# Gate and up products of the last block by seven quarter products in place of eight

## The chip, the cores and the metric

The kernel runs on one core of one Trainium2 chip. The metric is the device time in microseconds (us) of one execution. The engines are TensorE (PE; PEld is its weight load), VectorE (DVE), ScalarE (ACT), GpSimd (POOL), and SyncE (SP), which issues the transfers.

## The reference

A transformer layer runs over 2048 prompt tokens and 32 sample tokens; width 1024, hidden width 2816, all in fp32. The part that changes is the feed-forward network:

```python
x1 = _layer_norm(ALPHA * x + mix, ln1_g, ln1_b)
ffn = (jax.nn.silu(x1 @ w_gate) * (x1 @ w_up)) @ w_down
y = _layer_norm(ALPHA * x1 + ffn, ln2_g, ln2_b)
```

Attention, a pooling mix and the output projection come before it.

## The kernel before

**Blocks, pairs, chunks.** The 2048 prompt tokens are four blocks of 512 (BLOCKS, BW); the 32 sample tokens ride with the last block, whose width is 544 (XW). The hidden width is 22 chunks of 128 columns, taken two at a time: 11 pairs (PAIRS), each of chunks e = 0 and e = 1. For a block, x1T holds the transposed x1 (8 slices of 128 along the width, k = 0 to 7, times the tokens).

**Split operands.** TensorE multiplies fp32r numbers. Each fp32 operand is split in two: hi is ScalarE's copy of it, lo is raw minus hi, and a product is three matmuls, hi x hi, hi x lo, lo x hi. The raw tensor and its lo share one place. gate_hi (L1442) makes the hi of gate and up weights (tiles gw, four slots of [128, 8, 128]); gate_lo (L1819, VectorE) makes the lo of the gate weights and up_lo (L2173, GpSimd) that of the up weights; down_hi (L1447) and down_lo (L2178, GpSimd) do it for the down weights (dw, two slots).

**One pair in the last block on TensorE.** gate(b, p, e, g, i) issues the matmuls of gate (g = 0) or up (g = 1) for chunk e in four parts: 8 k, 2 halves of 272 tokens, 3 matmuls, so 48 of 128x272 each, into banks GU_BANK + g (first half) and Z_BANK + g (second). A pair is: gate e0; the ten down groups of the pair before (downs, into two banks that alternate; group d waits for the add of group d - 2); up e0; gate e1; up e1. A down group is 6 matmuls of 512 columns; the last two, for the packed sample tokens, have 4.

**What the other engines do for a chunk.** sigmoid (ScalarE, L1463) writes it to hT's raw; times_gate (L1827) and times_up (L1836) multiply by the two PSUM results (semaphores silu and prod); hidden_hi (L1470) and hidden_lo (L1845, L1847) split it; add_down (L1859) adds each down group to acc. Each is written into its engine's program at a fixed step of the pair; an engine executes its program in order. Up to the start of the last block's feed-forward part, attention and the mix of the next block run in the same steps (background); in the last block there are none. There the second normalization of the block before is spread over pairs 0 to 4: statistics and centring on VectorE (L1764), scaling on ScalarE (L1409), bias on GpSimd (L2154).

**Order of loads.** SyncE issues the gate and up loads (load_gate, 512 KB each) as their slot comes free, and both down loads of a pair after the down groups of the pair before.

**The end.** The last pair has no down groups; in it VectorE runs fold (L1767) and add_fold (L1771), which add up the sample rows. Then last_downs runs the down groups of the last two pairs together, and each tile of tokens is normalized as its sums are complete.

Of the kernel before, what the change touches and what calls it, by code (L numbers as in the profile page):

```python
# [23 lines left out]
P = 128  # L24
# [119 lines left out]
def stream(nc, ctx, sem, sb, passed, bank, ident, ident_r, mask, mask_r, maskd_r, eps_t, qT_d, kT_d, kcT_d, vp_d, vs_d, vc_d,  # L144
# [29 lines left out]
    acc = [sb(ctx, f"acc{u}", [P, BT, D]) for u in range(2)]  # L174
    acc_s = sb(ctx, "acc_s", [P, D])
# [64 lines left out]
    at[0] = 4 * D  # L240
    dw_last, hT_last = [], []
    for u in range(2):
        hi, lo = piece(f"dw_last_hi{u}", (D,)), piece(f"dw_last_lo{u}", (D,))
        dw_last.append([hi, lo, again(f"dw_last_raw{u}", (D,), F32)])
        hi, lo = piece(f"hT_last_hi{u}", (XW + DEC,)), piece(f"hT_last_lo{u}", (XW,))
        hT_last.append([hi, lo, again(f"hT_last_raw{u}", (XW,), F32)])

# [3 lines left out]
    def is_packed(b, p):  # L251
        return b == BLOCKS - 1 and p < PAIRS - 2

# [154 lines left out]
    def x_part(b, x):  # L408
# [43 lines left out]
        sem(f"f_{n}") for n in ("gate_up", "sig", "silu", "prod", "h_hi", "h_lo", "down", "sum"))  # L452
    y_stored, filled = sem("y_stored"), sem("filled")
    last_up, last_prod, last_hi, last_lo = (sem(f"last_{n}") for n in ("up", "prod", "hi", "lo"))
# [150 lines left out]
    def chunks(b):  # L605

        return [(0, BW)] if b < BLOCKS - 1 else [(0, XW // 2), (XW // 2, XW // 2)]

# [15 lines left out]
    with nc.Block() as block:  # L624
        @block.sync
        def _(sp):
# [175 lines left out]
            def load_gate(L):  # L802
# [3 lines left out]
                if P0:  # L806
# [9 lines left out]
            def load_down(b, p):  # L816
                if is_last(b, p):
                    sp.wait_ge(m_sums, mix_count(BLOCKS))
                    sp.wait_ge(folded, 2)
# [149 lines left out]
            for b in range(BLOCKS):  # L969
                for p in range(PAIRS):  # L970
                    pair = PAIRS * b + p
                    more = pair + 1 < PAIRS * BLOCKS
                    for i in range(4):
# [39 lines left out]
        def _(pe):  # L1013
# [196 lines left out]
            def gate(b, p, e, g, i):  # L1210
# [20 lines left out]
                if i == 1 and L == 4 * PAIRS * BLOCKS - 1:  # L1231
                    m.then_inc(last_up, 1)
# [78 lines left out]
            for b in range(BLOCKS):  # L1311
                for p in range(PAIRS):
                    if b + p == 0:
# [28 lines left out]
        def _(act):  # L1342
# [106 lines left out]
            def sigmoid(b, p, e):  # L1449
# [14 lines left out]
                m.then_inc(sig, 1)  # L1464

# [152 lines left out]
            for b in range(BLOCKS):  # L1618
                for p in range(PAIRS):
                    pair = PAIRS * b + p  # L1620
                    more = pair + 1 < PAIRS * BLOCKS
                    for i in range(4):
# [8 lines left out]
                    if p:  # L1631
                        for d in range(2 * tiles_of(b)):
                            background(next(slot))
                    for i in range(4):
# [6 lines left out]
                    for i in range(4):  # L1641
                        background(next(slot))
                        if i == 0 and more:
# [6 lines left out]
                    for i in range(4):  # L1650
# [5 lines left out]
                        if i == 3 and more:  # L1656
# [11 lines left out]
                else:  # L1668
                    for n, (first, w) in enumerate(chunks(b)):
                        if n == 0:  # L1670
                            act.wait_ge(last_prod, 1)
                        else:
                            act.wait_ge(prod, 2 * PAIRS * BLOCKS)
# [19 lines left out]
        def _(dve):  # L1693
# [136 lines left out]
            def times_up(b, p, e):  # L1830
# [6 lines left out]
                m.then_inc(prod, 1)  # L1837

# [489 lines left out]
```

## Time and profile before

| what | us |
|---|---|
| median of 3 runs | 2630.28 |
| lowest and highest | 2629.57, 2630.89 |
| the profiled execution, its own time | 2634.26 |
| its span, first to last instruction | 2632.5 |

Granted TensorE clock over the span: 0.995 of full. A profile shows one execution. Times in rows are us from the start of its span unless marked ns; "idle before <-releaser" is how long the engine had nothing to do before the instruction and what released it. L1227 is the line of the gate and up matmuls, L1259 that of the down matmuls.

### The profile page before, as it was taken

How to read it: one execution, taken by the hardware profiler on the slowest of the kernel's cores; microseconds unless marked ns; L12 is line 12 of the kernel's file. 1: busy time of each engine (PE TensorE's matmuls, PEld its weight loads, DVE VectorE, ACT ScalarE, POOL GpSimd, SP SyncE). 2: the span in 40 equal slices, each digit the busy share in tenths (PEclk: the TensorE clock that was granted, in tenths of full speed). 3: DMA queues.
4: the chain of work that ended last, by engine and by line, in shares of the span. 5: the costliest groups of instructions: out<-in, count | busy, mean ns of one | idle time of the engine just before them, and what ended most of it. 6: DMA issues, size and time to landing. Idle time of an engine off the chain costs nothing.

```text
span 2632.5 us, 37813 instructions
## 1 busy us (share of the span) xinstructions
PE 2559.2 (97%) x14210; PEld 2189.4 (83%) x14210; DVE 1470.4 (56%) x1952; ACT 1115.3 (42%) x1892; POOL 1126.4 (43%) x1013
## 2 busy tenths in 40 slices
PE   8999899999999999999999999999999999999998
PEld 8978798788878878778788887878878888999997
DVE  3366336666444366787734567787774354543335
ACT  4365326565232135566532265656554123322213
POOL 3465436755223135456621274556543124242223
PEclk9999999999999999999999999999999999999999
DMA  6697956764446233444254234333524512223222
GB/s 227 191 271 248 330 176 193 222 212 127 133 131 232 82 111 109 124 113 120 77 201 155 89 113 116 101 116 101 167 74 144 176 62 97 89 73 128 89 81 83
DMA packets 211013, 373.92 MB, mean 142 GB/s; under 512 B 30768, under 2 KB 105136, under 8 KB 208784
## 3 DMA queue, kind: packets, MB, share of 16 engines
q1 hardware_dynamic: 210832, 371.50, 44.7%
q8 instruction: 114, 1.87, 0.3%
q14 instruction: 67, 0.55, 0.1%
HBM read 303.34 MB, written 68.09 MB: 141 GB/s over the span
## 4 chain that ended last, share of the span: by engine, by line
PE 84%; DVE 5%; issue 3%; DMA 3%; POOL 2%; ACT 2%; SPq 1%; ACTq 0%; POOLq 0%; DVEq 0%
PE bank L1227 35%; PE bank L1259 19%; PE bank L1177 8%; PE bank L1136 7%; PE bank L1036 5%; PE bank L1083 4%; PE bank L1052 4%; DMA gw_lo_raw<-in_w_in_dram 2%; DVE left L1725 1%; PE bank L1159 1%; POOL gw_lo L2187 1%; DMA v_st<-v_cache_scratch 1%; DMA mixT<-mixT_scratch 0%; ACT bank L1375 0%; ACT beta L1374 0%
## 5 line engine op out<-in xcount | busy, mean ns | idle before, releaser
L1227 PE MATMUL bank<-x1T,gw_hi 128*128 128x512 f32 (+1 forms) x3488 | 930.2, 355 | 4.8 <-DVE hT_lo_raw L1827 3.4
L1227 PEld LDWEIGHTS bank<-x1T,gw_hi 128*128 128x128 f32 x3488 | 600.7, 189 | 85.9 <-issue 4.5
L1227 PE MATMUL bank<-x1T,gw_lo 128*128 128x512 f32 (+1 forms) x1744 | 614.4, 352 | 0.0
L2146 POOL TENSOR_TENSOR beta<-beta,left 128x512 f32<-128x512 f32 (+2 forms) x326 | 350.0, 1074 | 362.6 <-DVE left L1725 361.9
L2173 POOL TENSOR_TENSOR gw_lo<-gw_lo_raw,gw_hi 128x1024 fp32r<-128x1024 f32 x88 | 223.6, 2540 | 588.3 <-ACT gw_hi L1442 588.1
L1725 DVE TENSOR_TENSOR_SCAN left<-bank,left,zero_t 128x512 f32<-128x512 f32 (+2 forms) x326 | 363.9, 1116 | 74.7 <-ACT bank L1375 69.1
L1177 PE MATMUL bank<-x1T,gw_hi 128*128 128x256 f32 (+2 forms) x1472 | 355.7, 334 | 13.9 <-DVE x1T L1946 8.8
L1227 PEld LDWEIGHTS bank<-x1T,gw_lo 128*128 128x128 f32 x1744 | 328.4, 188 | 46.9
L1859 DVE TENSOR_TENSOR acc<-bank,acc 128x512 f32<-128x512 f32 x312 | 213.6, 686 | 260.4 <-PE bank L1259 260.1
L1365 ACT ACTIVATE aT<-bank 128x512 fp32r<-128x512 f32 (+2 forms) x326 | 173.7, 533 | 434.1 <-PE bank L1052 385.3
L1716 DVE TENSOR_TENSOR aT<-bank,aT 128x512 fp32r<-128x512 f32 (+2 forms) x326 | 196.9, 604 | 202.5 <-ACT aT L1365 201.1
L1259 PE MATMUL bank<-dw_hi,hT_hi 128*128 128x512 f32 x728 | 295.1, 405 | 8.7 <-issue 7.3
L2178 POOL TENSOR_TENSOR dw_lo<-dw_lo_raw,dw_hi 128x1024 fp32r<-128x1024 f32 x86 | 212.4, 2470 | 201.0 <-ACT dw_hi L1447 200.9
L1259 PE MATMUL bank<-dw_lo,hT_hi 128*128 128x512 f32 x728 | 287.2, 394 | 0.0
L1177 PEld LDWEIGHTS bank<-x1T,gw_hi 128*128 128x128 f32 x1472 | 245.2, 191 | 34.4 <-issue 11.7
L1259 PE MATMUL bank<-dw_hi,hT_lo 128*128 128x512 f32 x692 | 273.4, 395 | 0.0
L1463 ACT ACTIVATE hT_lo_raw<-bank 128x512 f32<-128x512 f32 (+1 forms) x106 | 53.3, 522 | 481.8 <-PE bank L1259 368.8
L1177 PE MATMUL bank<-x1T,gw_lo 128*128 128x256 f32 (+2 forms) x736 | 243.3, 331 | 0.0
L1036 PE MATMUL bank<-k_st,q_st 128*128 128x512 f32 (+3 forms) x688 | 215.5, 383 | 8.9 <-DVE left L1725 6.9
L2187 POOL TENSOR_TENSOR gw_lo<-gw_lo_raw,gw_hi 128x1024 fp32r<-128x1024 f32 x58 | 142.1, 2450 | 191.8 <-ACT gw_hi L1483 185.8
L1136 PE MATMUL bank<-wo_hi,mixT 128*128 128x256 f32 x1056 | 204.3, 285 | 3.8 <-DMA mixT<-mixT_scratch 3.7
L1083 PE MATMUL bank<-aT,v_st 128*128 128x512 f32 (+3 forms) x640 | 185.3, 371 | 0.0
(177 smaller groups left out, 3749.4 us busy)
## 6 DMA issues: line engine op xcount, KB each, us to landing
gw_lo_raw<-in_w_gate_dram SPq DMA_DIRECT2D x88, 512.0 KB, 3.6
gw_lo_raw<-in_w_up_dram SPq DMA_DIRECT2D x88, 512.0 KB, 3.6
dw_lo_raw<-in_w_down_dram SPq DMA_DIRECT2D x86, 512.0 KB, 4.4
gw_lo_raw<-in_w_in_dram SPq DMA_DIRECT2D x64, 512.0 KB, 4.5
k_st<-kT_scratch SPq DMA_DIRECT2D x160, 128.0 KB, 4.0
v_st<-v_scratch SPq DMA_DIRECT2D x80, 256.0 KB, 4.2
q_st<-qT_scratch SPq DMA_DIRECT2D x128, 128.0 KB, 3.9
wo_raw<-in_w_out_dram SPq DMA_DIRECT2D x16, 1024.0 KB, 5.6
```

Source lines behind the costliest of these rows:

```text
L1036: m = pe.matmul(z, q_st[queries.slot][:, j, who * P:(who + 1) * P], k_st[slot][:, 0:it.width], start=h == 0 and j == 0, stop=last)
L1083: m = pe.matmul(out[:, cols], v_st[held[0].slot][:, u - it.macro, :], aT[u % 2][j][:, cols], start=opens_group(u) and j == 0, stop=closes_ ...
L1136: x = pe.matmul(bank[Z_BANK + j % 2][:, 0:QW], turned[a][:, k, cols_of(t)], weights[c % 2][w][:, k, :], start=k == 0 and a + w == 0, stop= ...
L1177: y = pe.matmul(p_bank(b, n, slice(first, first + w)), weight[:, k, :], x1T[j][:, k, first:first + w], start=k == 0 and x == 0, stop=k == ...
L1227: m = pe.matmul(gu_bank(g, n)[:, 0:w], gw[L % 4][a][:, k, :], x1T[x][:, k, first:first + w], start=k == 0 and s == 0, stop=k == KD - 1 and ...
L1259: m = pe.matmul(bank[D_BANK + index % 2][0:cols.stop - cols.start, :], hid(b, p)[e][a][:, cols], dws(b, p)[e][w][:, half * 512:half * 512 ...
L1716: dve.tensor_tensor(aT[u % 2][1][:, cols], bank[t_at[u]][:, cols], r32(aT[u % 2][0][:, cols]), ALU.subtract).then_inc(aT_lo, 1)
L1725: dve.tensor_tensor_scan(out[:, 0:w][:, ::-1], bank[z_at[n]][:, 0:w][:, ::-1], zero_t[:, 0:1].broadcast_to([P, w]), out[:, w:w + 1], ALU.m ...
L1859: m = dve.tensor_tensor(x, bank[D_BANK + index % 2][:], x, ALU.add)
L2146: pool.tensor_tensor(x[:, 0:w], x[:, 0:w], left[n % RL][:, 1:w + 1], ALU.mult).then_inc(a_done, 1)
L2173: pool.tensor_tensor(gw[L % 4][1][:], gw[L % 4][2][:], r32(gw[L % 4][0][:]), ALU.subtract).then_inc(u_lo, 1)
L2178: pool.tensor_tensor(lo[:], raw[:], r32(hi[:]), ALU.subtract).then_inc(d_lo, 1)
```

## The change

In the last block, pairs 2 to 10 (WINO_FROM = 2; 18 chunks, c = 0 to 17), gate and up of a chunk are computed together as one product of two-by-two blocks: the width of 1024 is cut in TOP and LOWER (4 k each), the tokens in FIRST and SECOND (272 each), and the two outputs are gate and up. Strassen's scheme in Winograd's form takes seven quarter products (4 k x 3 = 12 matmuls of 128x272) instead of eight.

- Sums of weights, on VectorE in fp32 (quarter_sums, 4 instructions of 512 elements a row; one overwrites the top half of the up weights). Three of them fill a new tile, extra. Four weight operands become seven, so per chunk extra_hi (ScalarE, 1536 elements) and extra_lo (VectorE, 1536) are new. The lo of the gate weights goes from VectorE to GpSimd (gate_quarters_lo), except chunk 0's.
- Sums of tokens, once: token_sum, 8 instructions of 4 x 272 elements in pairs 0 and 1, and four splits (tokens_hi, tokens_lo), in part written over x1T.
- Sums of results, on VectorE, PSUM and SBUF to either: copy_part (ScalarE), make_v, make_y, make_up_2, make_up_1, make_gate_2, 272 elements each. Two of the seven products add up on top of others in a bank by accumulation.
- Sigmoid and the multiplies go by halves of 272. Six banks rotate (wino_bank).
- Order on TensorE: seven products of chunk e0, the ten down groups, seven products of e1. In VectorE's program extra_lo(c+1) stands after the add of down group 1, quarter_sums(c+2) after that of group 5, extra_lo(c+2) after that of group 8.
- The last pair's down weights move to where block 2's acc was; load_gate waits on the product that last reads the slot.

```diff
+            def seven_products(c):
+                pe.wait_ge(wg_lo, c + 1)
+                pe.wait_ge(prod, done - 1)
+                quarter(wino_bank(c, GATE_1), g, 0, x1T, 0, FIRST, True).then_inc(seven, 1)
+                pe.wait_ge(wx_lo, c + 1)
+                pe.wait_ge(t_lo, 3)
+                quarter(wino_bank(c, UP_2), s2, 0, xt[2], 0, whole, True).then_inc(seven, 1)
+                pe.wait_ge(wu_lo, c + 1)
+                pe.wait_ge(silu, done)
+                quarter(wino_bank(c, UP_1), u, 0, xt[3], 0, whole, True).then_inc(seven, 1)
+                pe.wait_ge(t_lo, 4)
+                pe.wait_ge(prod, done)
+                quarter(wino_bank(c, GATE_2), s1, 0, x1T, 0, SECOND, True).then_inc(seven, 1)
+                pe.wait_ge(part_copied, c + 1)
+                quarter(wino_bank(c, GATE_1), g, KH, x1T, KH, FIRST, False).then_inc(seven, 1)
+                pe.wait_ge(corner, 5 * c + Y_MADE)
+                quarter(wino_bank(c, UP_1), u, KH, xt[4], 0, whole, False).then_inc(seven, 1)
+                pe.wait_ge(corner, 5 * c + UP_2_MADE)
+                quarter(wino_bank(c, GATE_2), s4, 0, x1T, KH, SECOND, False).then_inc(seven, 1)
...
+            def quarter_sums(c):
+                dve.tensor_tensor(s1, u[:, TOP, :], u[:, LOWER, :], ALU.add).then_inc(s_sums, 1)
+                dve.tensor_tensor(u[:, TOP, :], g[:, TOP, :], u[:, TOP, :], ALU.subtract).then_inc(s_sums, 1)
+                dve.wait_ge(s_sums, 4 * c + S_1)
+                dve.tensor_tensor(s2, s1, g[:, TOP, :], ALU.subtract).then_inc(s_sums, 1)
+                dve.wait_ge(s_sums, 4 * c + S_2)
+                dve.tensor_tensor(s4, g[:, LOWER, :], s2, ALU.subtract).then_inc(s_sums, 1)
```

VectorE's program for a pair:

```diff
+            def wino_pair(b, p):
+                if c:
+                    make_gate_2(c - 1)
+                    half_times_gate(c - 1, 1)
+                    half_times_up(c - 1, 1)
+                else:
+                    times_up(b, p - 1, 1)
+                    tokens_lo(1, 3)
+                make_v(c)
+                hidden_lo(b, p - 1, 1)
+                make_y(c)
+                make_up_2(c)
+                quarter_sums(c + 1)
+                make_up_1(c)
+                make_gate_2(c)
+                for d in range(2 * tiles_of(b)):
+                    if not is_last(b, p):
+                        add_down(b, p - 1, d)
+                    if d == 1:
+                        extra_lo(c + 1)
+                    if d == 3:
+                        for group in range(4):
+                            for i in range(4):
+                                second_norm(b, p, group, i)
+                    if d == 5 and not is_last(b, p):
+                        quarter_sums(c + 2)
+                    if d == 8 and not is_last(b, p):
+                        extra_lo(c + 2)
+                if is_last(b, p):
+                    dve.wait_ge(summed, downs_done(b, PAIRS - 3))
+                    fold(3)
+                    add_fold(3)
+                half_times_gate(c, 0)
+                half_times_gate(c, 1)
+                half_times_up(c, 0)
+                half_times_up(c, 1)
+                make_v(c + 1)
+                hidden_lo(b, p, 0)
+                make_y(c + 1)
+                make_up_2(c + 1)
+                half_times_gate(c + 1, 0)
+                make_up_1(c + 1)
+                half_times_up(c + 1, 0)
```

GpSimd's:

```diff
+            def wino_pair(b, p):
+                if c == 0:
+                    up_quarters_lo(0)
+                gate_quarters_lo(c + 1)
+                up_quarters_lo(c + 1)
+                for group in range(4):
+                    for i in range(4):
+                        second_norm(b, p, group, i)
+                if not is_last(b, p):
+                    gate_quarters_lo(c + 2)
+                    up_quarters_lo(c + 2)
+                for e in range(2):
+                    down_lo(PAIRS * b + p, e)
```

ScalarE's:

```diff
+            def wino_pair(b, p):
+                if c:
+                    half_sigmoid(c - 1, 1)
+                else:
+                    tokens_hi(1)
+                copy_part(c)
+                hidden_hi(b, p - 1, 1)
+                gate_quarters_hi(c + 1)
+                up_quarters_hi(c + 1)
+                extra_hi(c + 1)
+                for group in range(4):
+                    for i in range(4):
+                        second_norm(b, p, group, i)
+                if more:
+                    gate_quarters_hi(c + 2)
+                    up_quarters_hi(c + 2)
+                    extra_hi(c + 2)
+                half_sigmoid(c, 0)
+                half_sigmoid(c, 1)
+                copy_part(c + 1)
+                hidden_hi(b, p, 0)
+                down_hi(pair, 0)
+                down_hi(pair, 1)
+                half_sigmoid(c + 1, 0)
```

On GpSimd gate_quarters_lo(c) waits for the fourth sum of c (S_4), up_quarters_lo(c) for up_quarters_hi(c), which waits for the second (S_3); extra_hi(c) waits for the fourth, extra_lo(c) for extra_hi(c). In pair 1, quarter_sums(0) stands before times_gate of e1 on VectorE, and extra_lo(0) and gate_quarters_lo(0) near the end of the pair.

## Rows read from the trace of the kernel before

**Rows 1.** The page's first part: busy time, share of the span, count of each engine
```profile
PE 2559.2 (97%) x14210; PEld 2189.4 (83%) x14210; DVE 1470.4 (56%) x1952; ACT 1115.3 (42%) x1892; POOL 1126.4 (43%) x1013
```

**Rows 2.** The chain of waits, last block, in order: start, us, what
```profile
2503.97 13.13 PE bank L1259 x56
...
2517.10 24.11 PE bank L1227 x192
...
2596.52 27.92 PE bank L1259 x120
```

**Rows 3.** Timeline, VectorE and weight loads, down groups: start, us, what, idle before
```profile
2513.76 0.69 DVE L1859 TENSOR_TENSOR acc<-bank,acc 128x512 f32<-128x512 f32 x1 [0.70 <-PE bank L1259]
...
2515.15 0.69 DVE L1859 TENSOR_TENSOR acc<-bank,acc 128x512 f32<-128x512 f32 x1 [0.70 <-PE bank L1259]
...
2517.14 0.69 DVE L1859 TENSOR_TENSOR acc_s<-bank,acc_s 128x512 f32<-128x512 f32 x1 [0.35 <-PE bank L1259]
...
2515.90 0.19 PEld L1259 LDWEIGHTS bank<-dw_hi,hT_hi 128*128 128x128 f32 x1 [0.28 <-DVE acc L1859]
```

**Rows 4.** One line's instructions each: ns min/median/max, first and last start, shapes
```profile
L1819 DVE TENSOR_TENSOR gw_lo<-gw_lo_raw,gw_hi x88: 1171/1218/3422, 563.6 to 2574.9; 128x1024 fp32r<-128x1024 f32 x88
...
L1859 DVE TENSOR_TENSOR acc<-bank,acc x312: 655/691/695, 661.6 to 2618.9; 128x512 f32<-128x512 f32 x156
...
L1836 DVE TENSOR_TENSOR hT_lo_raw<-bank,hT_lo_raw x40: 428/436/442, 2225.3 to 2572.8; 128x272 f32<-128x272 f32 x40
...
L1442 ACT ACTIVATE gw_hi<-gw_lo_raw x42: 1044/1060/1064, 2212.2 to 2579.0; 128x1024 fp32r<-128x1024 f32 x42
...
L1463 ACT ACTIVATE hT_lo_raw<-bank x40: 391/396/399, 2219.3 to 2566.7; 128x272 f32<-128x272 f32 x40
```

**Rows 5.** Timeline, VectorE: two pairs of instructions that follow each other
```profile
2387.80 0.69 DVE L1845 TENSOR_TENSOR hT_lo<-hT_lo_raw,hT_hi 128x512 fp32r<-128x512 f32 x1 [0.73 <-ACT hT_hi L1470]
...
2388.41 0.19 DVE L1847 TENSOR_TENSOR hT_hi<-hT_lo_raw,hT_hi 128x32 fp32r<-128x32 f32 x1
...
2600.75 0.69 DVE L1859 TENSOR_TENSOR acc<-bank,acc 128x512 f32<-128x512 f32 x1 [2.81 <-PE bank L1259]
...
2601.47 0.69 DVE L1746 BATCH_NORM_STATS2 stats<-acc 128x6 f32<-128x512 f32 x1
```

**Rows 6.** Timeline, GpSimd (POOL), where it meets VectorE
```profile
562.57 1.09 POOL L2146 TENSOR_TENSOR beta<-beta,left 128x512 f32<-128x512 f32 x1 [4.42 <-DVE left L1725]
...
2265.06 2.41 POOL L2178 TENSOR_TENSOR dw_lo<-dw_lo_raw,dw_hi 128x1024 fp32r<-128x1024 f32 x1 [2.24 <-ACT dw_hi L1447]
...
2270.29 3.26 POOL L2178 TENSOR_TENSOR dw_lo<-dw_lo_raw,dw_hi 128x1024 fp32r<-128x1024 f32 x1 [2.82 <-ACT dw_hi L1447]
...
2309.89 2.40 POOL L2173 TENSOR_TENSOR gw_lo<-gw_lo_raw,gw_hi 128x1024 fp32r<-128x1024 f32 x1
...
2312.26 5.19 POOL L2154 TENSOR_TENSOR acc<-acc,bias 128x1024 f32<-128x1024 f32 x2
```

**Rows 7.** Timeline, VectorE (DVE), the same stretches and the last pair's fold
```profile
561.21 1.28 DVE L1725 TENSOR_TENSOR_SCAN left<-bank,left,zero_t 128x512 f32<-128x512 f32 x1 [0.29 <-ACT bank L1375]
...
2265.09 3.45 DVE L1764 SCALAR_TENSOR_TENSOR acc<-acc,mv,gain 128x1024 f32<-128x1024 f32 x1
...
2313.35 1.85 DVE L1845 TENSOR_TENSOR hT_lo<-hT_lo_raw,hT_hi 128x512 fp32r<-128x512 f32 x1 [0.72 <-ACT hT_hi L1470]
...
2315.13 2.37 DVE L1847 TENSOR_TENSOR hT_hi<-hT_lo_raw,hT_hi 128x32 fp32r<-128x32 f32 x1
...
2580.74 3.29 DVE L1771 TENSOR_TENSOR acc_s<-acc_s,low_rows 32x1024 f32<-32x1024 f32 x1
```

**Rows 8.** The page's DMA issues: KB each, median us from issue to landing
```profile
gw_lo_raw<-in_w_gate_dram SPq DMA_DIRECT2D x88, 512.0 KB, 3.6
```

**Rows 9.** Timeline, ScalarE, end of pair 1 of the last block
```profile
2268.58 0.69 ACT L1463 ACTIVATE hT_lo_raw<-bank 128x272 f32<-128x272 f32 x2 [3.60 <-PE bank L1227]
...
2269.15 1.06 ACT L1447 ACTIVATE dw_hi<-dw_lo_raw 128x1024 fp32r<-128x1024 f32 x1
```

More of the change, by code:

```diff
@@ L1230, in gate, with quarter @@
                     m.then_inc(gate_up, 1)
-                if i == 1 and L == 4 * PAIRS * BLOCKS - 1:
-                    m.then_inc(last_up, 1)
+            def quarter(out, weights, at_k, moving, at_x, cols, first):
+                for k in range(KH):
+                    for s, (a, x) in enumerate(((0, 0), (0, 1), (1, 0))):
+                        m = pe.matmul(out, weights[a][:, at_k + k, :], moving[x][:, at_x + k, cols],
+                                      start=first and k == 0 and s == 0, stop=k == KH - 1 and s == 2, skip_group_check=True)
+                return m
+            def seven_products(c):
+                pair, e, _ = chunk_of(c)
+                done = 2 * pair + e
+                g, u = gw[2 * e], gw[2 * e + 1]
+                s1, s2, s4 = ([extra[e][j][:, x, :, :] for j in range(2)] for x in range(3))
+                whole = slice(0, HW)
+                pe.wait_ge(wg_lo, c + 1)
[16 more added lines that the diff above has]
+                quarter(wino_bank(c, GATE_2), s4, 0, x1T, KH, SECOND, False).then_inc(seven, 1)
             def first_gate_and_up(i):
@@ L1655, in _ @@
                             down_hi(pair, 1)
-                        if i == 3 and more:
+                        if i == 2 and before_wino:
+                            up_quarters_hi(0)
+                            extra_hi(0)
+                        elif i == 3 and not before_wino:
                             gate_hi(4 * pair + 5)
@@ new lines, in make_gate_2, with half_of, half_times_gate @@
+            def make_gate_2(c):
+                dve.wait_ge(seven, 7 * c + P3)
+                dve.tensor_tensor(wino_bank(c, GATE_2), wino_bank(c, GATE_2), part[:], ALU.add).then_inc(corner, 1)
+            def half_of(c, half):
+                pair, e, _ = chunk_of(c)
+                return hid(*divmod(pair, PAIRS))[e][2][:, (FIRST, SECOND)[half]]
+            def half_times_gate(c, half):
+                h = half_of(c, half)
+                dve.wait_ge(half_sig, 2 * c + half + 1)
+                dve.tensor_tensor(h, wino_bank(c, (GATE_1, GATE_2)[half]), h, ALU.mult).then_inc((half_silu, silu)[half], 1)
@@ L2048, in _ @@
                             times_up(b, p, 0)
-                        if i == 1 and more:
+                        if i == 1 and not before_wino:
                             gate_lo(4 * pair + 4)
```

251 lines of the change are left out of this document (222 added, 29 removed).

## The prediction

> **What bounds the kernel now.** I read the page first: TensorE is busy for 97% of the span [rows 1]. Then the chain of waits over the last block, where the change lies: it is matmuls end to end, 24.11 us for the 192 gate and up matmuls of a pair, 13.13 us for the 56 down matmuls, to 2624.4 us, where the tail of normalization begins [rows 2]. So 0.1256 us a gate or up matmul (24.11 / 192), and any matmul taken out comes off the time, unless TensorE then waits. Third, the timeline of VectorE, ScalarE and GpSimd in one pair, for what the new work costs and between which matmuls it falls. A down group of six matmuls takes 1.39 us (2513.76 to 2515.15), and only the tenth waits: its weights came 0.06 us after the add two groups back ended, about 0.1 us of matmul went with it (what the sum below leaves), and its own add began 1.30 us after that add's end [rows 3]. That is about 0.15 us a pair (13.13 against 8 x 1.39 + 2 x 0.93), and the pattern I price the new stalls by.
>
> **What the change takes from TensorE.** Seven products of 12 matmuls stand for 96 matmuls: 84 x 0.1256 = 10.55 us a chunk, one product 1.507 us, 1.51 us less a chunk, 3.01 us a pair, 27.1 us over nine pairs. The matmul's shape and its weights' shape stay, so the row's price holds. Waits stand in front of all seven; down groups have one each and lose nothing by it [rows 3].
>
> **What it adds.** Prices [rows 4, 5]: a VectorE add or subtract of 1024 elements 1.22 us, of 512 0.69 us (the next instruction starts 0.08 to 0.09 us before its end, if it needs nothing from it; 0.03 us after it, if it does), so 1536 about 1.75 us (estimate, same slope); corner sums of 272 from PSUM 0.44 us; ScalarE 1.06 us for 1024, about 1.5 us for 1536, 0.4 us for 272. Per pair VectorE gets 8 quarter sums, 10 corner sums, two splits of 1536, and loses one gate split. ScalarE and GpSimd (now 6 splits of 2.4 us, some 14 us) have room in a pair of 37 us; VectorE, some 26 us, too. Loads land 3.6 us after issue [rows 8], and each has over 4 us. What matters is order.
>
> **Inside a pair, steady state.** Zero is the first product of chunk c (e = 0); products end at 1.51, 3.01, 4.52, 6.03, 7.53, 9.04, 10.55. The corner sums stay ahead: the end of the chunk before (last corner sum, sigmoid, two multiplies, 0.2 + 0.44 + 0.4 + 0.44 + 0.44 and latencies) is through at 2.1, wanted at 4.5; make_y ends at 5.2, wanted at 7.5; make_up_2 ends at 6.7, wanted at 9.0. quarter_sums(c+1) runs from 6.57: 0.60 + 0.60 + 0.72 + 0.69 = 2.61, to 9.18.
>
> Then ten down groups, from 10.55, with only two PSUM banks: group d cannot start before the add of group d-2.
> - After add 1, extra_lo(c+1), 1.75 us: add 1 starts at 2 x 1.39 + 0.20 = 2.98 behind the start of the groups, the split at 3.58, add 2 at 5.24 and ends at 5.93. Group 4 wants to start at 5.56: with 0.06, and the 0.1 of matmul, as in [rows 3], a stall of 0.53.
> - After add 5, quarter_sums(c+2), 2.61 us. From the end X of group 5: add 5 X+0.20 to X+0.89, sums from X+0.80 to E = X+3.41, add 6 to E+0.60; group 8 wanted to start at X+2.78 and does at E+0.77: 1.40.
> - The old wait of 0.15 before group 9 goes.
> Without anything else a pair so changes by -3.01 + 0.53 + 1.40 - 0.15 = -1.23 us.
>
> **The shared lock.** GpSimd and VectorE exclude each other where VectorE has two inputs in SBUF. At 2313.35 such a subtract met a GpSimd add begun at 2312.26: it took 1.85 us for 0.69 and ended at 2315.20, so the add let go 2.2 us after its start; the waiting second GpSimd add then got in before VectorE's next instruction, which took 2.37 us for 0.18 [rows 6, 7]. Adds from PSUM never show it: 655 to 695 ns in 312 of them, against up to 3422 ns for the split of the same kind from SBUF [rows 4]. So no two instructions overlap here, and the one that waits is next. The Trainium skill says this too (SBUF — State Buffer, section SBUF: two separate sides): an exclusive lock, whoever starts first keeps it for its whole instruction; the trace agrees, with these durations. By a reading in which both merely ran side by side, the sum would be the third rival's.
>
> Who meets whom: at E the fourth sum of c+2 frees GpSimd's gate_quarters_lo(c+2), 0.08 us later (561.21 + 1.28 to 562.57) [rows 6, 7]; its up_quarters_lo(c+2) follows 2.37 us behind (2309.89 to 2312.26): E+2.45. On VectorE add 6 ends at E+0.60, add 8 starts 1.30 later at E+1.90, extra_lo(c+2) at E+2.50. GpSimd is first by 0.05 us. A lead of 0.03 us was enough at 2265.06 against 2265.09: 3.45 us, 2.2 more than 1024 elements take [rows 4, 6, 7]. Then extra_lo(c+2) runs from E+2.45+2.2 = E+4.65 to E+6.4, add 9 to E+7.0, the two half_times_gate to E+7.69. TensorE began chunk c+1 at E+2.63, and its third product, which waits for silu of chunk c, wants to start at E+5.64 and does at E+7.86: 2.22. The pair is then -1.23 + 2.22 = +0.99 us. If VectorE comes first, the multiplies end at E+5.5 and this wait is nought: those are the bounds, and I take GpSimd first, by these rows. The other meetings are clear: extra_lo(c+1) at 14.13 finds up_quarters_lo(c+1) letting go at 13.84; down_lo and hidden_lo miss each other.
>
> **Once each.**
> - Pairs 3 and 4: a GpSimd bias add follows directly on up_quarters_lo(c+1), at 14.00, before extra_lo(c+1) at 14.13: 2.1 us each, and in pair 3 the third bias add still touches the quarter sums (0.1): +4.3. Bounds 0 and 8.6 (a second meeting in each).
> - Entry (pair 1 to 2): wg_lo of chunk 0 is VectorE's last work, behind extra_lo(0), behind extra_hi(0), behind up_quarters_hi(0), behind down_hi, which ended at 2270.2 [rows 9]. Clear of locks: 2270.2 + 1.0 + 1.5 + 1.66 + 1.22 = 2275.6, where the first product could start at 2274.4 (the sigmoid of the chunk began at 2268.58, 0.2 after the last matmul before [rows 9]; + 6.0): 1.2. The two down_lo (one at 2270.29 [rows 6]) and up_quarters_lo(0) fall among quarter_sums, centre and extra_lo: up to three holds of 2.2, so 1.2 to 7.8; I take two, 5.6. The token sums lie in stretches with over 3 us of VectorE idle and cost nothing; were they late, add 1 or add 6 of pair 1 would be by up to 0.5.
> - Last pair: no down groups between its chunks, so the cover is gone. The gate split of c+1, moved to GpSimd, starts at 9.26 and ends at 11.66, wanted at 10.55: 1.3. extra_lo waits for it to 11.46, ends at 13.2; up_quarters_lo, waiting, holds to 15.3; then fold 0.7 and add_fold about 1.25 (3.29 before, which I read as a hold of 2.0 [rows 7]; an estimate) and two multiplies to 18.1, where product 3 wants 14.84: 3.4. So -3.01 + 4.7 = +1.7. Without locks -0.8.
> - The end: first columns' last_lo is ready 0.6 us after the last product, wanted 2.8 us after; the other half 3.5 against 11. Nothing.
>
> **Sum:** 8 pairs x 0.99 = 7.9, + 4.3 + 5.6 + 1.7 = +19.5 us. On the profiled execution, span 2632.5 us and 2634.26 us as a time: 2652.0 and 2653.8. The median of the runs is 4.0 lower, 2630.28; there 2649.8.
>
> **Rivals.**
> 1. VectorE first at E+2.5 in all pairs: 8 x -1.23 = -9.8, + 11.6: +1.8, 2632.1. Against it only 0.05 us of lead, worked out from latencies of 0.01 us grain. If it flips from pair to pair, anything between.
> 2. More meetings than I placed (both bias adds twice, three holds at the entry, hidden_lo behind a down_lo): 7.9 + 8.6 + 7.8 + 1.7 = +26, with one hold more in a few pairs +30: 2660.
> 3. Faster: the lock doesn't take these instructions (operands of [P, 4, 128] slices, or a hold much under 2.2 us). Place: every SBUF split and sum. 8 x -1.23 + 1.2 - 0.8 = -9.4: 2620.9. It decides from a hold of under about 0.1 us at E+2.45; [rows 6, 7] speak against it.
> 4. TensorE waits nowhere: -27.1, 2603.2. Needs VectorE's 2.61 us of sums to fit in 0.5 us of slack before group 8. Almost excluded.
>
> **How the numbers follow.** Forecast 0.55; rival 1 0.20; rival 2 0.10; rival 3 0.12; rival 4 0.03. 0.2% (5.3 us) is about what this kernel's runs can tell from no change. Slower: 0.55 + 0.10 + 0.03 of rival 1 = 0.68; faster: 0.12 + 0.03 = 0.15; within: 0.17. The range, 2627 to 2656, leaves out rivals 3 and 4 and most of 2 and takes in rival 1; the forecast's own is 2643 to 2656 (entry and bias adds at their bounds).
>
> **What would show it.** Per quarter product 12 matmuls in 1.5 us. A wait of TensorE for VectorE before groups 4 and 8 of each pair, some 0.5 and 1.4 us. VectorE's 1536-element split after the ninth add at 3.9 us where the other of the pair takes 1.75, and TensorE's third product of odd chunks released by the multiply of the even one. A pair of 38.2 us; 36.0 if rival 1 is right. I am wrong if that split is at 1.75 us throughout, or if GpSimd's second split starts after it.

## The result and the profile after

Before: 2630.28 us median (2629.57 to 2630.89). After: 2645.66 us median of five (2639.09 to 2648.51). The ratio of the executions is 1.0054, 95% interval 1.0039 to 1.0070: slower. Between the medians it is 15.4 us, where +19.5 was forecast.

The profiled execution of after is the fastest of the five, 2639.09 us. Its page, first part:

```profile
span 2637.2 us, 37777 instructions
...
PE 2541.1 (96%) x13994; PEld 2166.2 (82%) x13994; DVE 1583.2 (60%) x2127; ACT 1156.8 (44%) x1932; POOL 1186.9 (45%) x1030
```

Against [rows 1] TensorE has 216 matmuls fewer (18 x 12) and 18.1 us less work, VectorE 112.8 us more. 18 and not 27 us: a part of TensorE's time has become longer, some of it by a lower clock (below).

The chain of waits, last block, the matmul stretches in order: start, us, what. First three rows of the kernel before that [rows 2] lacks, then after's:

```profile
2213.23 30.14 PE bank L1227 x240
...
2256.48 24.11 PE bank L1227 x192
...
2554.33 42.19 PE bank L1227 x336
```

```profile
2208.19 30.13 PE bank L1285 x240
...
2276.12 12.16 PE bank L1293 x84
...
2303.21 21.22 PE bank L1293 x168
...
2342.91 21.23 PE bank L1293 x168
...
2381.26 21.23 PE bank L1293 x168
...
2526.00 21.23 PE bank L1293 x168
...
2562.16 21.23 PE bank L1293 x168
...
2601.28 27.88 PE bank L1347 x120
```

The block begins at 2213.2 before and at 2208.2 after, in code that the change doesn't touch; over all later runs it lies between 2209.9 and 2216.7. So I compare within the block (the last block's feed-forward part and the tail behind it), from its first row to the end of the span: 2632.5 - 2213.2 = 419.3 us before, 2637.2 - 2208.2 = 429.0 us after. This execution lost 9.7 us in the block, and the rows say where:

| stretch | before | after | lost |
|---|---|---|---|
| block start to first product of chunk 0 | 61.3 | 67.9 | +6.6 |
| first product of chunk 0 to that of chunk 2 | 37.23 | 37.7 | +0.5 |
| the next pair (3) | 37.23 | 39.70 | +2.5 |
| pair 4 | 37.23 | 38.35 | +1.1 |
| pairs 5 to 9 | 186.2 | 180.9 | -5.3 |
| last pair, first product to last downs | 24.11 | 28.51 | +4.4 |

(Before, 144 matmuls of each row of 192 or 336 belong to the pair before, so its starts are 2256.48 + 18.1 and 2554.33 + 18.1; 37.23 is a row of 24.11 and one of 13.13 in [rows 2]. After, a row of 168 is the odd chunk of one pair and the even one of the next, so the last pair begins at 2562.16 + 10.61 = 2572.77.)

What TensorE waited for, from its timeline of after: the entry (the first product, chunk 0's), the two groups of a steady pair, and the two waits of the last pair. The number in brackets is the idle time before, then what ended it:

```profile
2276.12 0.82 PE L1293 MATMUL bank<-x1T,gw_hi 128*128 128x272 f32 x2 [6.55 <-DVE gw_lo L2035]
...
2516.92 0.51 PE L1347 MATMUL bank<-dw_hi,hT_hi 128*128 128x512 f32 x1 [0.26 <-DVE acc L2175]
...
2523.89 0.50 PE L1347 MATMUL bank<-dw_hi,hT_hi 128*128 128x512 f32 x1 [1.12 <-DVE acc L2175]
...
2584.45 0.52 PE L1293 MATMUL bank<-x1T,gw_hi 128*128 128x272 f32 x2 [1.07 <-POOL gw_lo L2506]
...
2591.02 0.57 PE L1293 MATMUL bank<-xt_hi,gw_hi 128*128 128x272 f32 x1 [3.19 <-DVE hT_last_raw L2094]
```

Those at 2516.92 and 2523.89 are groups 4 and 8, where the prediction put them. No row has the multiply L2094 in front of the third product of an odd chunk: in this execution the wait that carried 17.8 of the forecast's 19.5 us didn't occur once. Here is the meeting in the pair of the second and third row, VectorE's and GpSimd's timelines:

```profile
2522.54 0.69 DVE L2029 TENSOR_TENSOR extra_raw<-gw_lo_raw,extra_raw 128x512 f32<-128x512 f32 x1
...
2525.72 1.75 DVE L2040 TENSOR_TENSOR extra_lo<-extra_raw,extra_hi 128x1536 fp32r<-128x1536 f32 x1
```

```profile
2523.37 2.41 POOL L2506 TENSOR_TENSOR gw_lo<-gw_lo_raw,gw_hi 128x1024 fp32r<-128x1024 f32 x1 [8.89 <-DVE extra_raw L2029]
2525.73 4.00 POOL L2511 TENSOR_TENSOR gw_lo<-gw_lo_raw,gw_hi 128x1024 fp32r<-128x1024 f32 x1
```

VectorE's extra_lo(c+2) starts 0.01 us ahead and runs its 1.75 us; GpSimd's up_quarters_lo(c+2) is recorded at 4.00 us for 2.40, because it waits. It is a tie, and all eight pairs of this execution are like it. GpSimd starts 0.14 us after the fourth sum's end (2523.23), where I had taken 0.08.

The table's rows hide one thing more, the granted clock. In these rows it is the number behind the POOL entry (1.00 is full); first around the entry, then around the last wait:

```profile
2262.00:2269.00 7.00, 7.00 (x58) 7.00 (x57) 6.65 (x5) 2.70 (x4) 6.34 (x3) 1.00 0.27 75
...
2276.00:2278.00 2.00, 1.88 (x8) 1.88 (x9) 1.96 (x4) 0.00 (x0) 0.00 (x0) 0.50 0.00 0
...
2280.00:2284.00 4.00, 4.00 (x34) 4.00 (x34) 1.79 (x5) 1.14 (x2) 0.00 (x0) 1.00 0.02 4
```

```profile
2591.00:2593.00 2.00, 1.98 (x9) 2.00 (x10) 1.62 (x4) 1.40 (x2) 0.00 (x0) 0.50 0.00 0
2593.00:2596.00 3.00, 3.00 (x15) 3.00 (x15) 0.46 (x2) 1.16 (x2) 2.72 (x2) 0.50 0.03 5
```

Behind its wait of 6.55 us TensorE came back at half clock, the lower of the two levels, 1.2 GHz: chunk 0's 84 matmuls took 12.16 us for 10.61, which is why the table's second row reads 37.7 for a steady 36.15. Behind the wait of 3.19 us it was at half until past 2596. The last pair took 28.51 us: 21.11 of products (as where nothing waits, below), 4.26 of the two waits, and 3.1 more, nearly all of it (some 2.7) from 5.5 us at half clock.

The clock also fell in pair 3. TensorE waited 2.45 us before down group 4, where a bias add held the split, and behind it groups 4 and 5 took 4.43 us. In the run with VectorE first (below) the same wait is there and the clock stays at full. After's chain, then that run's:

```profile
2332.45 4.43 PE bank L1347 x12
```

```profile
2335.38 3.07 PE bank L1347 x12
```

Pair 3 is 39.70 us here and 38.50 there, so the clock cost it 1.2 us. Nothing in the prediction accounts for any of the three.

### The profile page after: what moved, and what is told of

The parts are those of the page before. It is cut to its first block, busy times and chain, and to the rows that moved or that the text cites. A ratio compares the mean times of both kernels' runs of the same rounds, so it can differ in the third digit from the quotient of the medians.

```text
span 2637.2 us, 37777 instructions
## 1 busy us (share of the span) xinstructions
PE 2541.1 (96%) x13994; PEld 2166.2 (82%) x13994; DVE 1583.2 (60%) x2127; ACT 1156.8 (44%) x1932; POOL 1186.9 (45%) x1030
## 4 chain that ended last, share of the span: by engine, by line
PE 82%; DVE 7%; issue 4%; DMA 2%; POOL 2%; ACT 2%; SPq 0%; DVEq 0%; POOLq 0%; ACTq 0%
PE bank L1285 27%; PE bank L1347 17%; PE bank L1235 9%; PE bank L1194 7%; PE bank L1293 7%; PE bank L1094 5%; PE bank L1141 4%; PE bank L1110 4%; DVE left L1902 1%; DMA gw_lo_raw<-in_w_in_dram 1%; DVE acc L2175 1%; POOL gw_lo L2540 1%; PE bank L1217 1%; DMA v_st<-v_cache_scratch 1%; DMA mixT<-mixT_scratch 0%
## 5 line engine op out<-in xcount | busy, mean ns | idle before, releaser
L1285 PE MATMUL bank<-x1T,gw_hi 128*128 128x512 f32 (+1 forms) x2336 | 713.1, 389 | 4.8 <-DVE hT_lo_raw L2004 3.4
L1285 PEld LDWEIGHTS bank<-x1T,gw_hi 128*128 128x128 f32 x2336 | 419.3, 189 | 85.2 <-issue 4.5
L1285 PE MATMUL bank<-x1T,gw_lo 128*128 128x512 f32 (+1 forms) x1168 | 448.4, 384 | 0.0
L2500 POOL TENSOR_TENSOR gw_lo<-gw_lo_raw,gw_hi 128x1024 fp32r<-128x1024 f32 x70 | 181.7, 2595 | 427.6 <-ACT gw_hi L1537 427.4
L1235 PEld LDWEIGHTS bank<-x1T,gw_hi 128*128 128x128 f32 x1472 | 244.9, 190 | 32.9 <-issue 10.0
L1285 PEld LDWEIGHTS bank<-x1T,gw_lo 128*128 128x128 f32 x1168 | 220.1, 188 | 47.0
L2540 POOL TENSOR_TENSOR gw_lo<-gw_lo_raw,gw_hi 128x1024 fp32r<-128x1024 f32 x58 | 142.1, 2449 | 186.4 <-ACT gw_hi L1648 182.3
L1347 PEld LDWEIGHTS bank<-dw_hi,hT_hi 128*128 128x128 f32 x728 | 137.8, 189 | 61.8 <-DVE acc L2175 23.9
```

Of the source, the lines that this page charges most:

```text
L1235: y = pe.matmul(p_bank(b, n, slice(first, first + w)), weight[:, k, :], x1T[j][:, k, first:first + w], start=k == 0 and x == 0, stop=k == ...
L1285: m = pe.matmul(gu_bank(g, n)[:, 0:w], gw[L % 4][a][:, k, :], x1T[x][:, k, first:first + w], start=k == 0 and s == 0, stop=k == KD - 1 and ...
L1347: m = pe.matmul(bank[D_BANK + index % 2][0:cols.stop - cols.start, :], hid(b, p)[e][a][:, cols], dws(b, p)[e][w][:, half * 512:half * 512 ...
```

## The experiments

Beside each ratio to before I give the length of the last block in the profiled execution (419.3 before, 429.0 after). Chips and executions differ by a few us ahead of that block, so the block is the sharper measure of a place, and the ratio of the whole. The block is one execution each, though, and holds whatever the clock did in it. Behind the entry's wait alone that was 1.55 to 2.8 us in the seven profiles that have it. The first four runs below ran on one chip, the next four on another, the last on a third; each ratio is to the kernel before on the same chip.

### The changed kernel once more

> The changed kernel once more, unchanged, for the spread of its executions. Theory A (a tie for the shared lock): in the profiled execution VectorE's extra_lo(c+2) and GpSimd's up_quarters_lo(c+2) began within 0.01 us of each other in every pair, and VectorE had the lock each time; each lost tie costs 2.2 us, eight ties an execution, so the executions lie between 2639 and 2657 us, as they did (2639.1 to 2648.5), and differ by several us. Theory B (the spread has another cause: transfers, the clock, the stages before the last block): the same spread here, and it stays when the tie is removed.

Measured: 2649.05 us (2642.72 to 2656.34, six runs), ratio 1.0059, 1.0043 to 1.0074. Block 436.1 us, 7.1 more than in the first profile. One group of TensorE's lines in the last block:

```profile
L1293 PE MATMUL bank<-xt_hi,gw_hi 128*128 128x272 f32 x144 | 43.4, 301 | 9.7 <-DVE hT_lo_raw L2094 6.5 <-DVE hT_last_raw L2094 3.2
```

The 6.5 us for hT_lo_raw are three waits of 2.17, the wait of the forecast at its forecast price (2.22), but in three pairs of eight. In one of them both engines are recorded at the same hundredth:

```profile
2573.01 4.02 DVE L2040 TENSOR_TENSOR extra_lo<-extra_raw,extra_hi 128x1536 fp32r<-128x1536 f32 x1
```

```profile
2573.01 2.40 POOL L2511 TENSOR_TENSOR gw_lo<-gw_lo_raw,gw_hi 128x1024 fp32r<-128x1024 f32 x1
```

This time GpSimd got the lock and VectorE's 1.75 us became 4.02. Same program, other winner: by an estimate of eight times 2.17, that puts up to 17 us of chance on top of the few us by which executions of the kernel before differ too (2629.91 to 2637.53 in 19 runs of this chip).

### The tie decided for VectorE, and for GpSimd

For VectorE, in GpSimd's program:

```diff
                     gate_quarters_lo(c + 2)
+                    pool.wait_ge(wx_lo, c + 3)
                     up_quarters_lo(c + 2)
```

> GpSimd's up_quarters_lo(c+2) waits until extra_lo(c+2) is done, so VectorE is always first; no work is removed. Theory A: all executions near the fastest of the changed kernel, 2639 us, within 1.5 us of each other, ratio to before 1.0033. Theory B: median still about 2645 and a spread of 9 us.

For GpSimd, in VectorE's program:

```diff
                     if d == 8 and not is_last(b, p):
+                        dve.wait_ge(wu_lo, c + 3)
                         extra_lo(c + 2)
```

> VectorE's extra_lo(c+2) waits until up_quarters_lo(c+2) is done, so GpSimd is always first. Theory A: the third product of each odd chunk of pairs 2 to 9 starts some 2.4 us late (2.2 of the lock and 0.2 more, since the wait is for the end and not for the release), 8 x 2.4 = 19 us over the run before: 2658 us, small spread. Theory B: no more than the changed kernel's own 2645, since the slack behind the split hides it.

Measured, VectorE first: 2641.54 us (2639.19 to 2646.49, seven runs), ratio 1.0031, 1.0021 to 1.0041, block 428.0. GpSimd first: 2670.23 us (2665.31 to 2675.56, four runs), ratio 1.0132, 1.0117 to 1.0147, block 457.1. The first has the expected ratio (1.0033), and its interval and that of the undecided kernel don't meet. But its executions spread over 7.3 us, not 1.5: undecided it was 13.6 us, and the kernel before has 7.6 on this chip, so some 6 us of the spread point to the tie (few executions), and the rest has another cause. The second went the expected way but cost 28.7 us over the first, not the 19 expected of eight waits, and it spread over 10 us, not little. Its lines, its chain in two successive pairs, and the granted clock behind the wait at 2482.17:

```profile
L1293 PE MATMUL bank<-xt_hi,gw_hi 128*128 128x272 f32 x144 | 43.3, 301 | 21.8 <-DVE hT_lo_raw L2094 18.6 <-DVE hT_last_raw L2094 3.2
```

```profile
2443.42 18.34 PE bank L1293 x144
...
2482.17 19.86 PE bank L1293 x144
```

```profile
2481.00:2482.00 1.00, 0.00 (x0) 0.00 (x0) 1.00 (x4) 0.00 (x0) 0.00 (x0) 1.00 0.11 41
2483.00:2484.00 1.00, 1.00 (x7) 1.00 (x6) 0.63 (x2) 1.00 (x2) 0.00 (x0) 0.50 0.09 25
```

Eight waits make 18.6 us, 2.31 to 2.36 each. Behind five of the eight the 144 matmuls that follow took 19.86 to 19.88 us for 18.34: the clock fell to half, 1.52 us more each, 7.6 in all. That is 26.2 of the block's 29.1 us over the first run. So between its two forced orders a pair of instructions that starts as a tie is worth 1% of the kernel, and its price is the wait and, in some of the cases, the clock. If the cost grows evenly from one forced order to the other, the changed kernel itself (1.0054 and 1.0059, between 1.0031 and 1.0132) loses the tie in about two pairs of eight, an estimate; its two profiles show none and three.

### VectorE's work spread over the downs

The parts of extra_lo(c+1) stand behind adds 1, 2 and 3, the quarter sums of c+2 singly behind adds 4 to 7, and extra_lo(c+2) behind make_up_2(c+1), ahead of which the split isn't needed.

```diff
-                    if d == 1:
-                        extra_lo(c + 1)
+                    if d in (1, 2, 3):
+                        extra_lo_part(c + 1, d - 1)
...
-                    if d == 5 and not is_last(b, p):
-                        quarter_sums(c + 2)
-                    if d == 8 and not is_last(b, p):
-                        extra_lo(c + 2)
+                    if d in (4, 5, 6, 7) and not is_last(b, p):
+                        quarter_sum(c + 2, d - 4)
...
                 make_up_2(c + 1)
+                if not is_last(b, p):
+                    extra_lo(c + 2)
```

> Same work, other order on VectorE in the down groups: extra_lo(c+1) in three parts behind adds 1, 2, 3, the four quarter sums of c+2 one each behind adds 4, 5, 6, 7, extra_lo(c+2) behind make_up_2(c+1). Each gap of 1.39 us then holds an add and one instruction of 0.6 us. Theory A' (the lost time inside a pair is two back-to-back bursts of VectorE work against two PSUM banks): the stalls before groups 4 and 8 go, a pair takes 14 x 1.507 + 13.0 = 34.1 us against 36.15, 8 x 2.0 = 16 us less than 2639: 2623 us, a little more for the lock in pairs 3 and 4. Rival C (VectorE's or GpSimd's total of added work is the bound, whatever the order): 2639 or above.

Measured: 2628.05 us (2623.82 to 2632.16, eleven runs), ratio 0.9978, 0.9969 to 0.9986, block 414.1: 13.9 us less than with VectorE first, where 16 was expected. Pairs 3 and 4 made part of the difference: there the parts of extra_lo met the bias adds (2.88 and 2.27 us for 0.68), and the pairs lost 4.5 and 1.65 us over the steady one, 2.35 and 2.20 with VectorE first. The chain in steady state:

```profile
2452.86 21.11 PE bank L1293 x168
2473.96 13.10 PE bank L1347 x56
2487.06 21.11 PE bank L1293 x168
2508.17 13.10 PE bank L1347 x56
```

A pair is 34.21 us and TensorE waits for nothing. Against this, the changed kernel's steady 36.15 says that its two stalls cost 1.94 us a pair (0.54 at group 4, a wait of 0.26 and two groups in 3.07 us for 2.79; the other 1.40 at group 8), and 37.23 before says that the seven products save 3.02.

### Three single places

All three on top of the VectorE-first kernel (ratio 1.0031, block 428.0). The bias adds one a pair, behind extra_lo(c+1), in pairs 3 to 6:

```diff
-                if b and (p, group, i) in SHIFT_AT:
-                    affine(ln_index(2, b - 1), SHIFT_AT.index((p, group, i)))
+                at = SHIFT_AT if b < BLOCKS - 1 else [(q, 0, 2) for q in (3, 4, 5, 6)]
+                if b and (p, group, i) in at:
+                    affine(ln_index(2, b - 1), at.index((p, group, i)))
...
+                if 3 <= p <= 6:
+                    pool.wait_ge(wx_lo, c + 2)
```

> Compared with the run that holds GpSimd's second half behind VectorE's extra_lo(c+2) (1.0031 of before): the same with one GpSimd bias add a pair in pairs 3 to 6, behind extra_lo(c+1), in place of three in pair 3 and one in pair 4 at the downs' beginning; the rows are stored in pair 7. My theory: extra_lo(c+1) of pairs 3 and 4 takes 3.9 us instead of 1.75 because bias adds sit on the lock, and this stretches these pairs by 3.5 and 2.2 us over the steady 36.15. Expected: both pairs fall to 36.2 to 36.8, the time falls by 4.5 to 6 us, to 1.0008 to 1.0014 of before. Rival: the bias adds only use time in which the adds wait anyway (pairs 5 and 6 then pay what 3 and 4 save): under 1 us, 1.0028 to 1.0034.

Pair 1's down_lo behind up_quarters_lo(0), and left out at their old place:

```diff
                 if c == 0:
+                    pool.wait_ge(wg_lo, 1)
                     up_quarters_lo(0)
+                    for e in range(2):
+                        down_lo(WINO_PAIR - 1, e)
```

> Compared with the run that holds GpSimd's second half behind VectorE's extra_lo(c+2) (1.0031 of before): the same, but in pair 1 GpSimd makes both down_lo behind up_quarters_lo(0), which waits for VectorE's gate_quarters_lo(0). My theory: the 6.5 us in which TensorE waits for chunk 0's first low gate quarters come from VectorE's quarter sums, which alternate with GpSimd's passes for the shared lock (2.9 and 2.7 us in place of 0.6 and 0.7). Expected: the three sums back at 0.6 to 0.7 us each, TensorE's wait at the entry 0 to 2 us, the time lower by 4.5 to 6.5 us, 1.0007 to 1.0014 of before. Rival 1: the entry is bound by the arrival of the weights, and the wait falls by under 1.5 us (1.0026 to 1.0031). Rival 2: the late down_lo holds back pair 1's downs, and what the entry gains is lost at once (1.0030 to 1.0040).

The fold of the last pair later:

```diff
-                if is_last(b, p):
-                    dve.wait_ge(summed, downs_done(b, PAIRS - 3))
-                    fold(3)
-                    add_fold(3)
                 half_times_gate(c, 0)
...
                 make_up_2(c + 1)
+                if is_last(b, p):
+                    dve.wait_ge(summed, downs_done(b, PAIRS - 3))
+                    fold(3)
+                    add_fold(3)
```

> Compared with the run that holds GpSimd's second half behind VectorE's extra_lo(c+2) (1.0031 of before): the same, but in the last pair the fold and its add stand behind make_up_2(c+1) in place of in front of half_times_gate(c, 0). My theory: TensorE's 3.2 us wait in the last pair is the fold (2.76) and its add (1.22) in front of the half that frees the bank. Expected: that wait falls to 0 to 0.5 us, the time by 2.4 to 3.2 us, 1.0019 to 1.0023 of before. Rival: extra_lo(c+1) alone (2.2 us or more, in front of the same half) is what holds it: the wait stays above 2 us and the time falls by under 1.2 us (1.0027 to 1.0031).

| edit | median, lowest to highest, runs | ratio, interval | block | against 428.0 |
|---|---|---|---|---|
| bias adds | 2639.61, 2632.89 to 2643.19, 12 | 1.0023, 1.0015 to 1.0032 | 422.7 | -5.3 |
| down_lo | 2637.91, 2631.94 to 2641.81, 11 | 1.0017, 1.0007 to 1.0026 | 422.6 | -5.4 |
| fold | 2637.39, 2635.73 to 2638.56, 11 | 1.0017, 1.0009 to 1.0026 | 424.0 | -4.0 |

By the ratios each edit gained 2 to 4 us, less than expected for the first two. Each ratio's interval is some 2.5 us either way and the difference of two of them is good to about 3.5 (an estimate), so no edit's gain is settled by the ratios; what is shown is what happened at each place in the trace. The blocks are the expected size for the first two and above it (2.4 to 3.2) for the third. About 1 us of the first and the third is the clock behind the entry's wait, which neither edit touches: 12.38 and 12.35 us for chunk 0's products, 13.33 with VectorE first. Here is the changed kernel's own profile at the two first places. Pair 4, VectorE and GpSimd:

```profile
2367.57 3.95 DVE L2040 TENSOR_TENSOR extra_lo<-extra_raw,extra_hi 128x1536 fp32r<-128x1536 f32 x1
```

```profile
2367.51 2.39 POOL L2481 TENSOR_TENSOR acc<-acc,bias 128x1024 f32<-128x1024 f32 x1
```

The entry, VectorE's sums and GpSimd's passes:

```profile
2262.70 2.50 DVE L2024 TENSOR_TENSOR extra_raw<-gw_lo_raw 128x512 f32<-128x512 f32 x1 [0.32 <-DMA gw_lo_raw<-in_w_up_dram]
...
2265.72 2.88 DVE L2027 TENSOR_TENSOR extra_raw<-extra_raw,gw_lo_raw 128x512 f32<-128x512 f32 x1
2268.64 2.73 DVE L2029 TENSOR_TENSOR extra_raw<-gw_lo_raw,extra_raw 128x512 f32<-128x512 f32 x1
```

```profile
2261.39 3.25 POOL L2531 TENSOR_TENSOR dw_lo<-dw_lo_raw,dw_hi 128x1024 fp32r<-128x1024 f32 x1 [3.57 <-ACT dw_hi L1542]
2265.30 2.75 POOL L2531 TENSOR_TENSOR dw_lo<-dw_lo_raw,dw_hi 128x1024 fp32r<-128x1024 f32 x1 [0.66 <-ACT dw_hi L1542]
2268.01 2.81 POOL L2511 TENSOR_TENSOR gw_lo<-gw_lo_raw,gw_hi 128x1024 fp32r<-128x1024 f32 x1
```

Three sums of 0.7 us take 2.5 to 2.9 each, one behind each pass of GpSimd: three holds, where the forecast's sum took two. With the bias adds moved, pairs 3 and 4 are 36.15 and 36.21 us, for 38.50 and 38.35 in the kernel with VectorE first, and pairs 5 and 6 stay at 36.2: -4.5 of the 5.3. With down_lo moved, the three sums that had waited are at 0.69, TensorE's 6.55 us are gone but for 0.95 and 1.25 at two products, and the clock stays full. With the fold moved, the last pair:

```profile
L1293 PE MATMUL bank<-xt_hi,gw_hi 128*128 128x272 f32 x144 | 42.2, 293 | 0.5 <-POOL gw_lo L2511 0.5
```

3.2 us became 0.5, and the pair shortened by 4.1: the rest is again the clock, which stays at 1.00 here. That the clock doesn't fall behind every such wait is shown by the run with down_lo moved, whose last pair has the same wait (3.19 us) and a granted clock of 1.00 behind it; behind the same wait the kernel with VectorE first was at 0.52 for 3 us, the changed kernel at 0.50 for 5.

### All together

The spread order with the three edits:

> The spread version (extra_lo(c+1) in thirds, the quarter sums singly behind adds 4 to 7, extra_lo(c+2) behind make_up_2(c+1); 0.9978 of before) with the three edits of the other runs of this call on top. By the spread version's own trace the pairs in steady state are at 34.2 us, TensorE's matmuls alone, so that the three places are all that is left: entry 6.5, pair 3 1.66, the last pair 5.0. If they add: entry -5.5, bias adds -1.7, fold -2.5, together -8 to -11 us, 0.9937 to 0.9949 of before. If they are hidden behind one another: under -4 us, above 0.9963.

Measured: 2619.66 us (2618.33 to 2624.76, five runs), ratio 0.9956, 0.9943 to 0.9969, block 404.9, 9.2 less than the spread order alone. The ratio lies above the expected 0.9937 to 0.9949, its interval reaches into it (the medians alone give 0.9949); the block is as expected. What the expectation calls pair 3, 1.66 us, is pair 4 of the spread run; pair 3 had lost 4.5. What still held pairs 3 to 6, VectorE and GpSimd:

```profile
2365.83 2.32 DVE L2025 TENSOR_TENSOR extra_raw<-gw_lo_raw 128x512 f32<-128x512 f32 x1
```

```profile
2365.20 2.40 POOL L2496 TENSOR_TENSOR acc<-acc,bias 128x1024 f32<-128x1024 f32 x1 [3.56 <-DVE extra_lo L2042]
```

So one more version moves the bias add behind the pair's down_lo, and the last pair's quarter sums ahead of make_v:

```diff
+                if is_last(b, p):
+                    quarter_sums(c + 1)
                 make_v(c)
...
                 for e in range(2):
                     down_lo(PAIRS * b + p, e)
+                for group in range(4):
+                    for i in range(4):
+                        second_norm(b, p, group, i)
```

> The version with all three edits (0.9956 of before) with two changes that its own trace asks for. (1) GpSimd's bias add of pairs 3 to 6 stands behind the two down_lo of its pair, where GpSimd sat idle for 8.7 us, in place of in front of gate_quarters_lo(c+2), where it met one of VectorE's quarter sums (2.3 us for 0.7) and held each of these pairs at 35.33 instead of 34.21. (2) In the last pair the quarter sums of chunk 17 stand in front of make_v(16) instead of behind make_up_2(16), so that TensorE doesn't wait for GpSimd's low gate quarters (1.1) and VectorE's extra_lo (2.8 with its copy). My theory: the lock is free there and VectorE has slack between the products, so both are pure gains: pairs 3 to 6 at 34.2 (-4.5), the last pair -3 to -4, together -6.5 to -8.5 us, 0.9924 to 0.9932 of before. Rival: VectorE's low halves of the hidden (L2176) or extra_lo(c+2) meet the bias add at its new place and delay a bank's release: under -4 us, above 0.9941.

Measured: 2614.64 us (2613.05 to 2622.22, six runs), ratio 0.9933, 0.9921 to 0.9945, block 399.6, 5.3 less than the version before it, where 6.5 to 8.5 was expected. The first half did what it should: pairs 3 to 6 fell from 35.33 to 34.2 us, 4.5 us in all. The second gave 0.9 us in place of 3 to 4, because of one more meeting, VectorE and GpSimd:

```profile
2557.32 2.85 DVE L2179 TENSOR_TENSOR hT_lo<-hT_lo_raw,hT_hi 128x544 fp32r<-128x544 f32 x1
```

```profile
2557.20 2.39 POOL L2525 TENSOR_TENSOR gw_lo<-gw_lo_raw,gw_hi 128x1024 fp32r<-128x1024 f32 x1 [5.26 <-DVE extra_raw L2033]
```

The earlier sums free GpSimd's gate quarters 0.12 us ahead of hidden_lo, which stands in front of make_y, and TensorE waits 1.55 us for it.

## Why the prediction was right, and which terms were not

**By its own signs the forecast's case didn't occur in the first profile.** It called itself wrong if the 1536-element split after the ninth add is at 1.75 us throughout, and put a pair at 38.2 us, or 36.0 if rival 1 is right. In the profile of after the split is at 1.75 in all eight pairs and a steady pair is 36.15; in the second profile it is at 4.02 in three pairs. The step that failed is "GpSimd is first by 0.05 us".

**The sign held, in part by luck.** TensorE's saving was spent on waits, each at a place that the prediction names. The spread order shows it from the other side: with the same arithmetic and the waits of the steady pair gone, the kernel is faster than before. But with VectorE first in all pairs the sum was +1.8 us, less than the 5.3 that it takes for what these runs can tell from no change, and that run measured +8.7 in the block. Of the 6.9 us between them 4.5 are the clock (2.7 at the entry, 1.8 in the last pair), which the sum doesn't have.

**The products: right.** 3.01 us a pair forecast, 37.23 - 34.21 = 3.02 measured.

**The two stalls: right; the old wait: not.** 0.53 + 1.40 = 1.93 forecast, 1.94 measured. The 0.15 us that the old wait of [rows 3] was to give back isn't there: the ten down groups take 13.10 us without any wait and took 13.13 before [rows 2]. A pair with VectorE first is -1.08, not -1.23.

**The lock: price right, count wrong.** The lead of 0.05 us, on which the forecast and rival 1 parted, was worked out from a latency of 0.08 that is 0.14 here. What remains is a lead of 0.00 or 0.01 us that falls either way. The price was 2.22 and measured 2.17 in the changed kernel, 2.31 to 2.36 where it was forced. But it came up in none and in three of eight pairs, not in eight: 0 and 6.5 us in place of 17.8. It was the largest term of the sum.

**The bias adds: right.** 4.3 forecast; pairs 3 and 4 lie 3.55 and 2.2 over the steady 36.15, 5.75 in all, but 1.2 of it is the clock in pair 3. With VectorE first, where the clock stayed, it is 2.35 and 2.20, 4.55 in all.

**The entry: one hold short.** 5.6 forecast with two holds and 7.8 with three; there were three, as rival 2 had it, and 6.6 was lost.

**The last pair: its waits right, 4.7 against 1.07 + 3.19 = 4.26.** In place of +1.7 the pair lost 4.4, the difference being for the most part the clock.

**The missing term: the clock.** 1.55 us behind the entry's wait (12.16 for 10.61), 1.2 in pair 3, some 2.7 in the last pair, and 1.4 to 1.5 behind some of the lock waits. The forecast priced each wait at its own length. With the fold moved, it didn't fall in the last pair, which shortened by 4.1 us for a wait shorter by 2.7.

So that 2649.8 came within 4.2 us of 2645.66 is luck, errors of opposite sign: 11 to 18 us too much for the tie, 5.5 or more too little for the clock, and 2.5 too little for the entry (1.0), the bias adds (0.25) and the old wait (8 x 0.15). For the profiled execution these give 19.5 - 17.8 + 5.5 + 2.5 = 9.7, its block's loss. The case that occurred is neither the forecast's nor rival 1's, but the mixture that rival 1's last sentence allows, with the clock on top. Rival 3, that the lock doesn't take these instructions, is excluded by every meeting shown; rival 4 needed another order of VectorE's work, and even then comes to 414.1 us of block, 399.6 in the last version, not to 392.

What stays open: why the clock falls behind some waits of 2.2 to 3.2 us and not behind others of the same length, and what moves the block's start by up to 8.5 us between executions, which blurs every ratio here by a few us.

## What to carry to other kernels

Before an engine with 97% busy time is relieved, lay the added work of the others out against its waits, group by group: here 3.0 us a pair were won and 1.9 given back only because VectorE did 1.75 and 2.6 us of work in one piece each, between adds that two banks want every 1.39 us; cut in pieces of 0.7 us the same work cost a steady pair nothing. When two instructions that exclude each other come out within 0.1 us on paper, don't forecast a winner but order them, or move one to where the other engine works from PSUM, as the last version does with the bias add; a tie also makes the times spread. And a wait of TensorE of the lengths that occur here, 2.2 to 6.6 us, is priced with what the granted clock may lose behind it: 1.2 to 2.8 us in this kernel, when it falls.

## What the runs showed of the hardware

- At recorded starts 0.00 to 0.01 us apart either engine may get the lock, and the same program decides it differently from pair to pair and execution to execution. In after VectorE won even at 2489.57 against GpSimd's 2489.56. The loser is recorded from its issue: 4.02 us for 1.75, or 4.00 for 2.40.
- GpSimd lets go 0.13 us ahead of its recorded end, 2.27 us after its start: 2573.01 + 4.02 - 1.75 = 2575.28 against 2575.41, and in pair 4, against a bias add, the same (2367.57 + 3.95 - 1.75 = 2369.77 against 2369.90). In the entry each instruction that waited was the next to run, so that long passes of GpSimd and short ones of VectorE took turns.
- TensorE's granted clock fell from full to half behind the entry's wait of 6.55 us in all seven profiles that have it, and behind the last pair's of 3.19 in five of six. It fell behind five of twelve of 2.45 to 2.47 (pairs 3 and 4 of six profiles), five of eight of 2.31 to 2.36, one of three of 2.17, and behind the one of 2.16 in the last pair of the spread run, but not behind the same one in the version with the three edits. The matmuls behind a fall took 1.2 to 2.8 us longer. The Trainium skill (TensorE: Matmul & The Clock Gate, section What's actually happening) describes the same two levels and a fall after idle time; the trace agrees on both.
